# The dense mixer's down product with tokens held in the array and 512 weight columns moving, its sum copied, turned and added at the change of layers

## The chip, the core and the metric

The kernel runs on one core of one Trainium2 chip. The metric is the device time of one execution in microseconds (us). Below, PE is TensorE's matmul side and PEld its load of the operand that is held in the array, DVE is VectorE, ACT is ScalarE, POOL is GpSimd and SP the engine that issues most DMAs. Each engine runs its own instruction list in order; the lists meet only at semaphores (`wait_ge` waits for a count, `then_inc` raises one). Nothing overtakes a waiting instruction on its own engine.

## What is computed

Two residual layers over 256 tokens with 1024 channels; layer 0 ends in a dense SwiGLU, layer 1 in an expert SwiGLU. Cut to what matters here:

```python
D_MODEL, SEQ, DEPTH, D_FF = 1024, 256, 2, 2816

def swiglu(x, wg, wu, wd):
    return (jax.nn.silu(x @ wg) * (x @ wu)) @ wd

for layer in range(DEPTH):
    h = rmsnorm(x, norm1_g[layer])
    proj = h @ w_in[layer]            # the next layer begins with this
    ...                               # four mixers, gates, output projection
    h2 = rmsnorm(x, norm2_g[layer])
    f = swiglu(h2, ffn_wg, ffn_wu, ffn_wd) if layer % 2 == 0 else moe_ffn(...)
    x = x + f
```

The change is in `@ wd` of layer 0 and in the `x = x + f` behind it.

## The kernel before

**Data.** `x` lies in SBUF with channels on the 128 partitions: 8 tiles of 256 tokens, handled in four pairs (`PAIRS`). Weights come in units of 1 MB (128 x 2048), through three slots (`RING`). ACT copies a unit into a rounded part `weight_hi` (`split`, L441), DVE subtracts to get the rest `weight_lo` (`split`, L797). Activations are split into hi and lo in the same way, and a product is three matmuls (hi by hi, hi by lo, lo by hi), all recorded at L1525.

**The dense mixer** (`FF_STEPS` = 11 steps, three units each: gate, up, down). A step is `up_pair(4, ...)`, a down unit and `up_pair(6, ...)` on PE; nine of them are a loop, the last two are written out. ACT copies half of a gate or up sum out of PSUM (L652), DVE adds the other half (L1159), scales it (L1161), multiplies gate by up (L1172) and splits the product into `y_hi` (L1174) and `y_lo` (L800). `down(j)` then holds a 128 x 128 weight block in the array and moves the 256 tokens: 2 x 8 blocks x 3 = 48 matmuls of 256 columns a unit, summed over all steps in PSUM banks 0 to 3, two channel tiles to a bank. The units of the mixer are f0+0 to f0+32, the last two (f0+31, f0+32) both being down units.

**The change of layers.** In the last down unit (`down(..., final=True)`) the banks become ready one after another. DVE adds a bank to `x` (`added`, L938); ACT scales and rounds the pair for the next layer (`high`, L453) and squares it for the norm (`squares`, L458); DVE makes its lo part (`low`, L807), which raises `xg_lo_done`. PE begins the first unit of layer 1 (u = 0, `tile_pair` with `early` = 6), waiting for a count of `xg_lo_done` ahead of every second channel tile. The second unit (u = 1) needs `lo_done` of its weights: ACT's and DVE's splits of it are the last of the mixer's splits. In ACT's list its split stands ahead of the four `high`, in DVE's list behind the last `low`. Behind it DVE adds up the squares (`squares_added`, L814 and L815); PE sums them over partitions between u = 1 and u = 2 (`norm_sums`, a matmul of `proj` by `con`), and the norm's root and reciprocal follow (L463, L819).

**A step that exists already** is `merged_turned`: PE turns 128 x 128 blocks of an f32 tensor with tokens on partitions (`merged`, part of `proj`) by matmuls with the identity (`con`), L1622. It is used for the output projection. `wide_unit` is the product with tokens held and 512 weight columns moving, used in other units of the mixer layers.

Of the kernel before, what the change touches and what calls it, by code (L numbers as in the profile page):

```python
# [21 lines left out]
D = 1024  # L22
SEQ = 256
# [80 lines left out]
def trunk(nc, x_in, par_in, con_in, fin_in, mix_w, ff_w, moe_w, out, rows, made):  # L104
# [4 lines left out]
    with ctx:  # L109
# [164 lines left out]
        def hi_free(v, item):  # L274
# [18 lines left out]
            "y_done", "yz_done", "yb_sq_added", "yb_sum", "yb_std", "yb_recip", "yb_rstd", "ya_f", "ya_hi", "ya_lo", "yc_f",  # L293
            "yc_hi", "yc_lo", "yd_f", "yd_hi", "yd_lo", "yb_f", "yb_hi", "yb_lo", "early_ps", "gate_done", "early_added", "late_ps", "gate_b_done", "merge_done", "mT_ps",
            "m_hi", "m_lo", "half_copied", "g_scaled", "silu_done", "hid_done",
            "ff_bank", "y_bank", "xg_done", "xT_ps", "x_tok_done", "ssq_done", "pre_done",
# [136 lines left out]
        def _(act):  # L433
# [22 lines left out]
            def squares(q):  # L456

                A(flat(sq[:, 2 * q:2 * q + 2, :]), flat(x[:, 2 * q:2 * q + 2, :]), ACT.Square).then_inc(S["sq_done"], 1)  # L458
# [17 lines left out]
            def mixer_unit(layer, u, behind_split=None):  # L476
# [49 lines left out]
                elif U_PB + 2 <= u < U_OUT:  # L526
                    for q in (0, 1) if u == U_PB + 2 else (2, 3):
                        act.wait_ge(S["mT_ps"], PAIRS * layer + q + 1)
                        A(h_hi[:, 2 * q:2 * q + 2, :], tiles(bank(4 + q)), ACT.Copy).then_inc(S["m_hi"], 1)
                elif u > U_OUT and layer == 0:  # L530
                    high(1, u - U_OUT - 1)
                    squares(u - U_OUT - 1)
# [74 lines left out]
            for layer in range(DEPTH):  # L607
# [16 lines left out]
                else:  # L624
                    for q in range(PAIRS):
                        high(2 * layer, q)
                        squares(q)
                u = 0
# [9 lines left out]
                if layer == 0:  # L638
# [10 lines left out]
                    def half_copied(to, b, unit):  # L649

                        act.wait_ge(unit_used, RING + f0 + unit + 1)
                        A(tiles(to), PS[:, b:b + 2, 0:SEQ], ACT.Copy).then_inc(S["half_copied"], 1)  # L652

# [19 lines left out]
                    step(FF_STEPS - 2, True)  # L673
                    split(f0, FF_UNITS - 1 + AHEAD)

# [107 lines left out]
        def _(dve):  # L783
# [151 lines left out]

            def added(q):

                V.tensor_tensor(flat(x[:, 2 * q:2 * q + 2, :]), flat(x[:, 2 * q:2 * q + 2, :]), bank(q), ALU.add).then_inc(S["x_sum"], 1)  # L938

# [168 lines left out]
            for layer in range(DEPTH):  # L1108
# [38 lines left out]
                if layer == 0:  # L1147
# [8 lines left out]
                    def halves_scaled(out_, b, copied, signal, n):  # L1156

                        dve.wait_ge(S["half_copied"], copied)
                        V.tensor_tensor(tiles(out_), tiles(out_), PS[:, b:b + 2, SEQ:], ALU.add).then_inc(signal, 1)  # L1159
                        dve.wait_ge(signal, n + 1)  # L1160
                        V.tensor_tensor(tiles(out_), tiles(out_), rstd_pair, ALU.mult).then_inc(signal, 1)  # L1161
# [33 lines left out]
                    split(u + 2, AHEAD)  # L1195
                    for q in range(PAIRS):
                        if q < PAIRS - 1:
                            dve.wait_ge(S["ff_bank"], q + 1)
                        else:
                            dve.wait_ge(unit_used, RING + f0 + FF_UNITS)  # L1200
                        added(q)
                        if q:
                            low(2, q - 1)
                    low(2, PAIRS - 1)
                    split(u + 3, AHEAD)
# [317 lines left out]
        def _(pe):  # L1523
# [92 lines left out]
            def merged_turned(layer, n):  # L1616

                pe.wait_ge(S["merge_done"], TT * (HALVES * layer + n + 1))
                for k in range(4 * n, 4 * n + 4):
# [3 lines left out]
                    if k % 2:  # L1623
                        last.then_inc(S["mT_ps"], 1)

# [11 lines left out]
            def mixer_unit(layer, u):  # L1637
# [10 lines left out]
                elif u < IN_UNITS:  # L1648
# [9 lines left out]
                    elif layer == 0 and u == 1:  # L1658
                        pe.wait_ge(S["first_lo"], 4)
                        tile_pair(1, b, 1, a=xg, between=lambda n: split_is(1) if n == 0 else None)  # L1660
                    else:
                        tile_pair(u, b, u, (S["xg_lo_done"], 2 * PAIRS * layer) if u == 0 else None, 6 if u == 0 else KT, xg)
                elif u < U_GB:
# [160 lines left out]
            for layer in range(DEPTH):  # L1824
# [8 lines left out]
                if layer == 0:  # L1833
                    f0 = MIX_UNITS

                    def down(j, to=(hid_hi, hid_lo), final=False):

                        order = [(f, m) for f in range(2) for m in range(KT)]
                        if final:
                            order.sort(key=lambda fm: fm[1] // 2)  # L1840
                        for n, (f, m) in enumerate(order):
                            last = product(bank(m // 2)[:, (m % 2) * SEQ:(m % 2 + 1) * SEQ], (f0 + j) % RING, f * KT + m,
                                           to[0][:, f, :], to[1][:, f, :], False, False)
                            if final and n in (3, 7, 11):
                                last.then_inc(S["ff_bank"], 1)
                        last.then_inc(unit_used, 1)
# [23 lines left out]
                    pe.wait_ge(S["hid_done"], 5 * FF_STEPS - 5)  # L1870
                    down(u + 2)
                    split_is(f0 + u + 3)
                    pe.wait_ge(S["hid_done"], 5 * FF_STEPS)
                    down(u + 3, (last_hi, last_lo), True)

# [263 lines left out]
```

## Time and profile before

| | us |
|---|---|
| runs shown | 1823.03, 1823.12, 1824.83 (median 1823.12) |
| the profiled execution | 1824.91, its span 1823.0 |
| PE busy | 1809.2 (99%) |
| DVE, ACT busy | 1513.5 (83%), 1185.9 (65%) |
| dense mixer of layer 0 | about 342 to 522.8 |
| granted clock of TensorE, mean | 0.999 |

The span is from the first to the last recorded instruction; 1.9 us lie around it. Because matmuls overlap, the busy time of PE says little; what counts is the distance from the start of one matmul to the start of the next.

### The profile page before, as it was taken

The numbers are of one execution on the slowest core, as the hardware profiler recorded it, in microseconds if no ns is written. First come the engines' busy times: TensorE is split into PE (matmuls) and PEld (weight loads), VectorE is DVE, ScalarE is ACT, GpSimd is POOL, SyncE is SP. The second block draws the span as 40 slices with busy tenths as digits, with TensorE's granted clock in tenths as the row PEclk, the third lists the DMA queues.
The fourth block names the chain that finished last, engine by engine and source line by source line (L and its number), as shares of the span: only waits on it lengthen the run. The fifth ranks groups of instructions, "written<-read, shape, count | busy, mean of one in ns | idle before, by whom it ended". The sixth has DMA issues, their size and how long they took to land.

```text
span 1823.0 us, 25706 instructions
## 1 busy us (share of the span) xinstructions
PE 1809.2 (99%) x9443; PEld 1537.3 (84%) x9443; DVE 1513.5 (83%) x1372; ACT 1185.9 (65%) x1032; POOL 165.8 (9%) x143
## 2 busy tenths in 40 slices
PE   9999999999999999999999999999999999999997
PEld 7888888999998888879888888888888888888886
DVE  7887687866689867787989988898898898898897
ACT  5755554544456655656778777677677777777775
POOL 1044000000000350000920000000000000000010
PEclk9999999999999999999999999999999999999999
DMA  9554445555545454454999999999999999999994
GB/s 361 181 182 169 172 168 183 185 185 184 196 174 197 170 180 167 164 203 179 405 383 374 379 385 386 370 380 383 389 374 377 367 384 388 375 384 373 384 408 185
DMA packets 75229, 521.20 MB, mean 286 GB/s; under 512 B 8352, under 2 KB 8608, under 8 KB 14368
## 3 DMA queue, kind: packets, MB, share of 16 engines
q1 hardware_dynamic: 72112, 509.34, 74.1%
q0 software_dynamic: 2912, 11.01, 1.6%
q8 instruction: 42, 0.69, 0.1%
q14 instruction: 19, 0.16, 0.0%
q10 hardware_dynamic: 144, 0.00, 0.0%
HBM read 509.83 MB, written 10.49 MB: 285 GB/s over the span
## 4 chain that ended last, share of the span: by engine, by line
PE 96%; DVE 2%; DMA 1%; ACT 1%; issue 0%; ACTq 0%; SPq 0%; DVEq 0%
PE psum L1525 94%; PE psum L1999 1%; DMA weight_raw<-mix_w 0%; PE psum L1931 0%; DMA par<-par_in 0%; DVE yb_pair L807 0%; DVE weight_lo L797 0%; PE psum L1752 0%; PE psum L1622 0%; DVE rstd_row L819 0%; DVE proj L830 0%; DVE weight_lo L1104 0%; DVE h_pair L850 0%; DVE x L938 0%; ACT weight_hi L441 0%
## 5 line engine op out<-in xcount | busy, mean ns | idle before, releaser
L797 DVE TENSOR_TENSOR weight_lo<-weight_raw,weight_hi 128x2048 fp32r<-128x2048 f32 x139 | 319.9, 2302 | 107.0 <-ACT weight_hi L441 105.7
L441 ACT ACTIVATE weight_hi<-weight_raw 128x2048 fp32r<-128x2048 f32 x139 | 265.5, 1911 | 93.6 <-PE psum L1525 89.4
L1525 PE MATMUL psum<-weight_hi,y_hi 128*128 128x512 f32 x768 | 305.5, 398 | 0.6 <-DVE y_lo L1254 0.6
L1525 PE MATMUL psum<-weight_hi,y_lo 128*128 128x512 f32 x768 | 300.0, 391 | 0.0
L1525 PE MATMUL psum<-weight_lo,y_hi 128*128 128x512 f32 x768 | 298.9, 389 | 0.0
L1525 PE MATMUL psum<-weight_lo,y_lo 128*128 128x512 f32 x672 | 261.6, 389 | 0.0
L1525 PE MATMUL psum<-weight_raw_r,y_hi 128*128 128x512 f32 x576 | 224.6, 390 | 0.0
L1525 PE MATMUL psum<-proj_r,y_hi 128*128 128x512 f32 x576 | 224.3, 389 | 0.0
L1525 PE MATMUL psum<-h_pair,weight_hi 128*128 128x512 f32 (+1 forms) x928 | 203.2, 342 | 0.0
L850 DVE TENSOR_TENSOR weight_raw_r<-weight_raw,weight_lo 128x2048 fp32r<-128x2048 f32 x72 | 164.8, 2289 | 25.0 <-ACT weight_lo L474 24.7
L850 DVE TENSOR_TENSOR proj_r<-proj,weight_lo 128x2048 fp32r<-128x2048 f32 x72 | 164.9, 2290 | 24.5 <-ACT weight_lo L474 24.4
L1525 PE MATMUL psum<-weight_hi,h_pair 128*128 128x512 f32 x576 | 184.9, 393 | 0.0
L1525 PEld LDWEIGHTS psum<-h_pair,weight_hi 128*128 128x128 f32 x928 | 156.5, 190 | 17.6 <-issue 1.8
L1525 PEld LDWEIGHTS psum<-weight_hi,y_lo 128*128 128x128 f32 x768 | 144.1, 188 | 30.8
L850 DVE TENSOR_TENSOR weight_raw_r<-weight_raw,weight_hi 128x2048 fp32r<-128x2048 f32 x72 | 164.8, 2289 | 5.6 <-ACT weight_hi L474 5.2
L1525 PEld LDWEIGHTS psum<-weight_lo,y_hi 128*128 128x128 f32 x768 | 144.2, 188 | 29.9
L1525 PEld LDWEIGHTS psum<-weight_hi,y_hi 128*128 128x128 f32 x768 | 144.3, 188 | 28.8 <-DVE y_lo L1254 0.8
L850 DVE TENSOR_TENSOR proj_r<-proj,weight_hi 128x2048 fp32r<-128x2048 f32 x72 | 164.8, 2289 | 4.3 <-ACT weight_hi L474 4.2
L474 ACT ACTIVATE weight_hi<-weight_raw 128x2048 fp32r<-128x2048 f32 x72 | 138.2, 1920 | 30.0 <-DMA weight_raw<-moe_w 28.3
L474 ACT ACTIVATE weight_hi<-proj 128x2048 fp32r<-128x2048 f32 x72 | 138.8, 1927 | 20.8 <-DMA proj<-moe_w 17.8
L474 ACT ACTIVATE weight_lo<-weight_raw 128x2048 fp32r<-128x2048 f32 x72 | 137.7, 1912 | 19.9 <-DMA weight_raw<-moe_w 19.9
L1525 PEld LDWEIGHTS psum<-weight_lo,y_lo 128*128 128x128 f32 x672 | 126.1, 188 | 26.2
(316 smaller groups left out, 3115.6 us busy)
## 6 DMA issues: line engine op xcount, KB each, us to landing
proj<-moe_w SPq DMA_DIRECT2D x144, 1024.0 KB, 6.8
weight_raw<-moe_w SPq DMA_DIRECT2D x144, 1024.0 KB, 6.7
weight_raw<-mix_w SPq DMA_DIRECT2D x106, 1024.0 KB, 4.8
first_raw<-moe_w SPq DMA_DIRECT2D x48, 1024.0 KB, 6.7
weight_raw<-ff_w SPq DMA_DIRECT2D x33, 1024.0 KB, 4.7
made_rows<-zeros POOLq DMA_DIRECT2D x1, 4096.0 KB, 20.7
made_rows<-pool_tmp SPq DMA_DIRECT2D x8, 512.0 KB, 6.2
weight_raw<-mix_w SPq DMA_DIRECT2D x4, 512.0 KB, 8.5
```

The source lines that it names most:

```text
L441: A(hi[:, slot, :], raw[:, slot, :], ACT.Copy).then_inc(hi_done, 1)
L474: A(hi_e(v), raw_e(v), ACT.Copy).then_inc(hi_done, 1)
L797: V.tensor_tensor(lo[:, slot, :], raw[:, slot, :], hi[:, slot, :].bitcast(f32), ALU.subtract).then_inc(lo_done, 1)
L850: V.tensor_tensor(lo_e(v), raw_e(v), hi_e(v).bitcast(f32), ALU.subtract).then_inc(lo_done, 1)
L1525: return nc.tensor.matmul(o, a, b_, start=start, stop=stop, skip_group_check=True, **k)
L1999: last = nc.tensor.transpose(bank(6)[:, f * P:(f + 1) * P], ff_h[:, f * P:(f + 1) * P], C_("ident"))
```

## The change

The down product swaps its operands: a 128-token block of the hidden rows is held and 512 columns of the weights move, so a unit is 2 x 2 x 2 x 3 = 24 matmuls of 512 columns. The sum now has tokens on partitions, one bank for each half of the channels (`n`) and token block (`t`). So before `x` can take it, ACT copies each bank to SBUF (`ff_kept`), PE turns it in 16 blocks (`ff_turned`, eight at a time) into banks 4 to 7, and DVE adds from there. `ff_turned(0)` stands ahead of the last two parts of the last unit, `ff_turned(1)` inside the first unit of layer 1, which now has `early` = 4. In the last two units parts are interleaved. ACT's split of unit u = 1 of layer 1 moves behind the last `squares`. The semaphores `mT_ps` and `half_copied` are renamed.

```diff
@@ scalar, start of layer 1
-                    for q in range(PAIRS):
-                        high(2 * layer, q)
-                        squares(q)
+                    def ff_kept(n, t):
+                        if n and t:
+                            act.wait_ge(unit_used, RING + MIX_UNITS + FF_UNITS)
+                        else:
+                            act.wait_ge(S["ff_bank"], TT * n + t + 1)
+                        A(merged[:, t, cols(n)], bank(2 * n + t), ACT.Copy).then_inc(S["ff_copied"], 1)
+
+                    ff_kept(0, 0)
+                    ff_kept(0, 1)
+                    high(2, 0)
+                    ff_kept(1, 0)
+                    high(2, 1)
+                    ff_kept(1, 1)
+                    squares(0)
+                    squares(1)
+                    high(2, 2)
+                    high(2, 3)
+                    squares(2)
+                    squares(3)
+                    split(MIX_UNITS, FF_UNITS - 1 + AHEAD)
@@ scalar, end of the mixer
-                    split(f0, FF_UNITS - 1 + AHEAD)
@@ vector, end of the mixer
-                    for q in range(PAIRS):
-                        if q < PAIRS - 1:
-                            dve.wait_ge(S["ff_bank"], q + 1)
-                        else:
-                            dve.wait_ge(unit_used, RING + f0 + FF_UNITS)
-                        added(q)
-                        if q:
-                            low(2, q - 1)
-                    low(2, PAIRS - 1)
+                    for half in range(2):
+                        for q in (2 * half, 2 * half + 1):
+                            dve.wait_ge(S["turned_ps"], PAIRS + q + 1)
+                            added(q, 4)
+                        low(2, 2 * half)
+                        low(2, 2 * half + 1)
@@ tensor
+            def ff_turned(n):
+                pe.wait_ge(S["ff_copied"], 2 * FF_STEPS + TT * (n + 1))
+                for k in range(4 * n, 4 * n + 4):
+                    for t in range(TT):
+                        at = (k % 2) * SEQ + t * P
+                        last = nc.tensor.transpose(bank(4 + k // 2)[:, at:at + P], merged[:, t, k * P:(k + 1) * P], C_("ident"))
+                    if k % 2:
+                        last.then_inc(S["turned_ps"], 1)
@@ tensor, units of a mixer layer
+                    elif u == 0:
+                        tile_pair(0, b, 0, (S["xg_lo_done"], 2 * PAIRS * layer), 4, xg, lambda n: ff_turned(1) if n == 0 else None)
                     else:
-                        tile_pair(u, b, u, (S["xg_lo_done"], 2 * PAIRS * layer) if u == 0 else None, 6 if u == 0 else KT, xg)
+                        tile_pair(u, b, u, a=xg)
@@ tensor, the down unit
+                    def down_part(j, to, n, t):
+                        slot = (f0 + j) % RING
+                        for f in range(2):
+                            w = slice(f * D + 512 * n, f * D + 512 * n + 512)
+                            mm(bank(2 * n + t), to[0][:, f, token(t)], hi[:, slot, w], False, False)
+                            mm(bank(2 * n + t), to[0][:, f, token(t)], lo[:, slot, w], False, False)
+                            last = mm(bank(2 * n + t), to[1][:, f, token(t)], hi[:, slot, w], False, False)
+                        return last
@@ tensor, the last two down units
-                    down(u + 2)
+                    rows_a, rows_b = (hid_hi, hid_lo), (last_hi, last_lo)
+                    down_part(u + 2, rows_a, 0, 0)
+                    down_part(u + 2, rows_a, 0, 1)
+                    down_part(u + 2, rows_a, 1, 0)
                     split_is(f0 + u + 3)
                     pe.wait_ge(S["hid_done"], 5 * FF_STEPS)
-                    down(u + 3, (last_hi, last_lo), True)
+                    down_part(u + 3, rows_b, 0, 0).then_inc(S["ff_bank"], 1)
+                    down_part(u + 3, rows_b, 0, 1).then_inc(S["ff_bank"], 1)
+                    down_part(u + 2, rows_a, 1, 1).then_inc(unit_used, 1)
+                    ff_turned(0)
+                    down_part(u + 3, rows_b, 1, 0).then_inc(S["ff_bank"], 1)
+                    down_part(u + 3, rows_b, 1, 1).then_inc(unit_used, 1)
```

ACT's list at the change of layers, before: from the last copy of an up sum (L652) to the norm's table load. The row with x2 at L441 holds the splits of the first two units of layer 1.

```order
L652 ACTIVATE proj<-psum 128x512
L441 ACTIVATE weight_hi<-weight_raw 128x2048 x2
L453 ACTIVATE yb_pair<-x,par 128x256 x2
L458 ACTIVATE proj<-x 128x512
L453 ACTIVATE yb_pair<-x,par 128x256 x2
L458 ACTIVATE proj<-x 128x512
L453 ACTIVATE yb_pair<-x,par 128x256 x2
L458 ACTIVATE proj<-x 128x512
L453 ACTIVATE yb_pair<-x,par 128x256 x2
L458 ACTIVATE proj<-x 128x512
L441 ACTIVATE weight_hi<-weight_raw 128x2048 x2
L463 ACT_TABLE_LOAD
```

The same place of the changed kernel, where L670 is the copy of an up sum and L631 is `ff_kept`.

```order
L670 ACTIVATE proj<-psum 128x512
L441 ACTIVATE weight_hi<-weight_raw 128x2048
L631 ACTIVATE proj<-psum 128x512 x2
L453 ACTIVATE yb_pair<-x,par 128x256 x2
L631 ACTIVATE proj<-psum 128x512
L453 ACTIVATE yb_pair<-x,par 128x256 x2
L631 ACTIVATE proj<-psum 128x512
L458 ACTIVATE proj<-x 128x512 x2
L453 ACTIVATE yb_pair<-x,par 128x256 x4
L458 ACTIVATE proj<-x 128x512 x2
L441 ACTIVATE weight_hi<-weight_raw 128x2048 x3
L463 ACT_TABLE_LOAD
```

One of the two splits ahead of `high` has moved behind the last `squares`, and the second `high` stands behind the third `ff_kept`.

DVE's list at the same place, before (L797 split, L938 `added`, L807 `low`, L814 and L815 `squares_added`).

```order
L797 TENSOR_TENSOR weight_lo<-weight_raw,weight_hi 128x2048
L938 TENSOR_TENSOR x<-x,psum 128x512 x2
L807 SCALAR_TENSOR_TENSOR yb_pair<-x,par,yb_pair 128x256 x2
L938 TENSOR_TENSOR x<-x,psum 128x512
L807 SCALAR_TENSOR_TENSOR yb_pair<-x,par,yb_pair 128x256 x2
L938 TENSOR_TENSOR x<-x,psum 128x512
L807 SCALAR_TENSOR_TENSOR yb_pair<-x,par,yb_pair 128x256 x4
L797 TENSOR_TENSOR weight_lo<-weight_raw,weight_hi 128x2048
L814 TENSOR_TENSOR proj<-proj 128x512 x3
L815 TENSOR_TENSOR proj<-proj 128x256
L797 TENSOR_TENSOR weight_lo<-weight_raw,weight_hi 128x2048 x2
L819 RECIPROCAL rstd_row<-rstd_row 128x256
```

And of the changed kernel (L814 is the split there, L955 `added`, L824 `low`, L831 and L832 `squares_added`).

```order
L814 TENSOR_TENSOR weight_lo<-weight_raw,weight_hi 128x2048
L955 TENSOR_TENSOR x<-x,psum 128x512 x2
L824 SCALAR_TENSOR_TENSOR yb_pair<-x,par,yb_pair 128x256 x4
L955 TENSOR_TENSOR x<-x,psum 128x512 x2
L824 SCALAR_TENSOR_TENSOR yb_pair<-x,par,yb_pair 128x256 x4
L814 TENSOR_TENSOR weight_lo<-weight_raw,weight_hi 128x2048
L831 TENSOR_TENSOR proj<-proj 128x512 x3
L832 TENSOR_TENSOR proj<-proj 128x256
L814 TENSOR_TENSOR weight_lo<-weight_raw,weight_hi 128x2048 x2
L836 RECIPROCAL rstd_row<-rstd_row 128x256
```

The additions come in twos, and DVE's split of unit u = 1 keeps its place.

## Rows read from the trace of the kernel before

**Rows 1.** The page: busy times and shares; the chain that ended last, by engine.

```profile
PE 1809.2 (99%) x9443; PEld 1537.3 (84%) x9443; DVE 1513.5 (83%) x1372; ACT 1185.9 (65%) x1032; POOL 165.8 (9%) x143
...
PE 96%; DVE 2%; DMA 1%; ACT 1%; issue 0%; ACTq 0%; SPq 0%; DVEq 0%
```

**Rows 2.** Timeline of PE, dense mixer: start, length in us, engine, line, operation, tiles, count.

```profile
359.05 2.00 PE L1525 MATMUL psum<-yb_pair,weight_hi 128*128 128x512 f32 x8
...
370.22 0.28 PE L1525 MATMUL psum<-y_hi,weight_hi 128*128 128x256 f32 x1
...
375.98 2.00 PE L1525 MATMUL psum<-yb_pair,weight_hi 128*128 128x512 f32 x8
```

**Rows 3.** Timeline of PE, a `wide_unit` of layer 0, first and last of 24.

```profile
240.04 0.39 PE L1525 MATMUL psum<-weight_hi,y_hi 128*128 128x512 f32 x1
...
245.25 0.39 PE L1525 MATMUL psum<-weight_hi,y_lo 128*128 128x512 f32 x1
```

**Rows 4.** Timeline of PE around `merged_turned` of layer 0.

```profile
305.50 1.03 PE L1622 MATMUL psum<-con,proj 128*128 128x128 f32 x8
306.29 0.48 PE L1525 MATMUL psum<-weight_hi,yb_pair 128*128 128x512 f32 x1
306.60 0.40 PE L1525 MATMUL psum<-weight_lo,yb_pair 128*128 128x512 f32 x1
```

**Rows 5.** Timeline of ACT, first reader of the turned tiles.

```profile
306.13 1.09 ACT L529 ACTIVATE h_pair<-psum 128x512 fp32r<-128x512 f32 x2 [3.90 <-PE psum L1622]
```

**Rows 6.** Timeline of PE at the change of layers.

```profile
511.28 0.28 PE L1525 MATMUL psum<-y_hi,weight_hi 128*128 128x256 f32 x1
...
522.80 0.40 PE L1525 MATMUL psum<-yb_pair,weight_hi 128*128 128x256 f32 x2
...
524.53 0.51 PE L1525 MATMUL psum<-yb_pair,weight_hi 128*128 128x256 f32 x2
524.87 0.28 PE L1525 MATMUL psum<-yb_pair,weight_lo 128*128 128x256 f32 x1
...
534.71 0.59 PE L1525 MATMUL psum<-proj,con 128*128 128x256 f32 x2
```

**Rows 7.** Timeline of DVE at the change of layers.

```profile
514.75 0.69 DVE L800 TENSOR_TENSOR y_lo<-proj,y_hi 128x512 fp32r<-128x512 f32 x1
...
518.68 0.69 DVE L938 TENSOR_TENSOR x<-x,psum 128x512 f32<-128x512 f32 x1 [1.04 <-PE psum L1525]
...
520.72 0.87 DVE L807 SCALAR_TENSOR_TENSOR yb_pair<-x,par,yb_pair 128x256 fp32r<-128x256 f32 x2
...
525.46 2.28 DVE L797 TENSOR_TENSOR weight_lo<-weight_raw,weight_hi 128x2048 fp32r<-128x2048 f32 x1
527.66 2.14 DVE L814 TENSOR_TENSOR proj<-proj 128x512 f32<-128x512 f32 x3
...
530.18 4.49 DVE L797 TENSOR_TENSOR weight_lo<-weight_raw,weight_hi 128x2048 fp32r<-128x2048 f32 x2
537.18 1.75 DVE L819 RECIPROCAL rstd_row<-rstd_row 128x256 f32<-128x256 f32 x1 [2.52 <-ACT rstd_row L463]
```

**Rows 8.** Timeline of ACT at the change of layers.

```profile
511.48 0.60 ACT L652 ACTIVATE proj<-psum 128x512 f32<-128x512 f32 x1 [2.61 <-PE psum L1525]
...
517.29 1.92 ACT L441 ACTIVATE weight_hi<-weight_raw 128x2048 fp32r<-128x2048 f32 x1 [3.41 <-PE psum L1525]
519.46 0.91 ACT L453 ACTIVATE yb_pair<-x,par 128x256 fp32r<-128x256 f32 x2 [0.25 <-DVE x L938]
520.28 0.62 ACT L458 ACTIVATE proj<-x 128x512 f32<-128x512 f32 x1
```

**Rows 9.** DVE in the loop, the last split of a hidden product ahead of the down unit at 370.22.

```profile
368.19 0.69 DVE L800 TENSOR_TENSOR y_lo<-proj,y_hi 128x512 fp32r<-128x512 f32 x1
```

**Rows 10.** Stretches at the end: us, busy times (counts), granted clock, DMA share, GB/s.

```profile
1816.00:1818.00 2.00, 0.00 (x0) 0.00 (x0) 1.97 (x6) 1.37 (x5) 0.00 (x0) 1.00 0.00 0
1818.00:1820.00 2.00, 0.00 (x0) 0.00 (x0) 0.94 (x2) 1.13 (x2) 0.00 (x0) 0.60 0.31 116
```

**Rows 11.** DMA issues from 500 to 560: KB each, median us from issue to landing.

```profile
weight_raw<-mix_w SPq DMA_DIRECT2D x10, 1024.0 KB, 4.8
```

More of the change, by code:

```diff
@@ L293, in trunk @@
             "y_done", "yz_done", "yb_sq_added", "yb_sum", "yb_std", "yb_recip", "yb_rstd", "ya_f", "ya_hi", "ya_lo", "yc_f",
-            "yc_hi", "yc_lo", "yd_f", "yd_hi", "yd_lo", "yb_f", "yb_hi", "yb_lo", "early_ps", "gate_done", "early_added", "late_ps", "gate_b_done", "merge_done", "mT_ps",
-            "m_hi", "m_lo", "half_copied", "g_scaled", "silu_done", "hid_done",
+            "yc_hi", "yc_lo", "yd_f", "yd_hi", "yd_lo", "yb_f", "yb_hi", "yb_lo", "early_ps", "gate_done", "early_added", "late_ps", "gate_b_done", "merge_done", "turned_ps",
+            "m_hi", "m_lo", "ff_copied", "g_scaled", "silu_done", "hid_done",
             "ff_bank", "y_bank", "xg_done", "xT_ps", "x_tok_done", "ssq_done", "pre_done",
@@ L527, in mixer_unit @@
                     for q in (0, 1) if u == U_PB + 2 else (2, 3):
-                        act.wait_ge(S["mT_ps"], PAIRS * layer + q + 1)
+                        act.wait_ge(S["turned_ps"], 2 * PAIRS * layer + q + 1)
                         A(h_hi[:, 2 * q:2 * q + 2, :], tiles(bank(4 + q)), ACT.Copy).then_inc(S["m_hi"], 1)
@@ L651, in half_copied @@
                         act.wait_ge(unit_used, RING + f0 + unit + 1)
-                        A(tiles(to), PS[:, b:b + 2, 0:SEQ], ACT.Copy).then_inc(S["half_copied"], 1)
+                        A(tiles(to), PS[:, b:b + 2, 0:SEQ], ACT.Copy).then_inc(S["ff_copied"], 1)
                     def step(i, last):
@@ L934, in into_experts, with added @@
                 last.then_inc(S["xg_done"], 1)
-            def added(q):
-                V.tensor_tensor(flat(x[:, 2 * q:2 * q + 2, :]), flat(x[:, 2 * q:2 * q + 2, :]), bank(q), ALU.add).then_inc(S["x_sum"], 1)
+            def added(q, first=0):
+                V.tensor_tensor(flat(x[:, 2 * q:2 * q + 2, :]), flat(x[:, 2 * q:2 * q + 2, :]), bank(first + q), ALU.add).then_inc(S["x_sum"], 1)
             def stage(name, layer):
@@ L1156, in halves_scaled @@
                     def halves_scaled(out_, b, copied, signal, n):
-                        dve.wait_ge(S["half_copied"], copied)
+                        dve.wait_ge(S["ff_copied"], copied)
                         V.tensor_tensor(tiles(out_), tiles(out_), PS[:, b:b + 2, SEQ:], ALU.add).then_inc(signal, 1)
@@ L1623, in merged_turned @@
                     if k % 2:
-                        last.then_inc(S["mT_ps"], 1)
+                        last.then_inc(S["turned_ps"], 1)
[6 more added lines that the diff above has]
+                    if k % 2:
+                        last.then_inc(S["turned_ps"], 1)
             def out_half(layer, q, n):
@@ L1834, in _, with down @@
                     f0 = MIX_UNITS
[L1836 to L1845, printed above, removed]
+                    def down_part(j, to, n, t):
[6 more added lines that the diff above has]
+                        return last
+                    def down(j):
+                        for n in range(2):
+                            for t in range(TT):
+                                last = down_part(j, (hid_hi, hid_lo), n, t)
                         last.then_inc(unit_used, 1)
```

## Prediction

> **What bounds the kernel.** I read the page first: PE is busy 99% of the span, and the chain that ended last lies 96% on PE [rows 1]. That leaves open whether PE waits between its matmuls, so I read its timeline in the mixer. One turn of the loop is 359.05 to 375.98, 16.93 us. The down unit fills 370.22 to 375.98: 5.76 us for 48 matmuls, 0.120 us from start to start, and the next up product follows at once [rows 2]. PE waits for nobody in the loop, so what shortens its list there shortens the kernel, as long as the others keep up. They do: the hidden product of the down unit at 370.22 is ready at 368.19 + 0.69 = 368.88, 1.3 us early [rows 9], and it is timed from the up product in front of it, which does not change.
>
> The second place to read is the change of layers, because the changed sum has to pass three engines there. From the start of the second-last down unit, 511.28, to the norm's sum behind unit u = 1, 534.71, PE takes 23.43 us [rows 6]. That is four units of 5.76 and about 0.4 of waiting and restart at 524.53. I take 511.28 as zero in what follows, and the norm's sum as the end of the place, since all later work of DVE and ACT on layer 1 is timed from it.
>
> **The matmuls.** Before, a down unit costs 5.76 us. After, it is 24 matmuls of 512 columns with tokens held. The trace has this form in `wide_unit`: 24 of them, the first at 240.04 and the last at 245.25, so 5.21 / 23 = 0.2265 us from start to start [rows 3]. A unit is 5.44, a saving of 0.32 us. Nine down units are in the loop: **-2.9 us**. The other two are in the place that I work out as a whole. All eleven would be -3.5.
>
> The Trainium skill (TensorE: Matmul & The Clock Gate, "Back-to-back issue gap") gives N / 2.4 + 2.5 ns for isolated matmuls, 109 and 216 ns, by which a unit would go from 5.24 to 5.18 us, an estimate from that page. The trace disagrees: it shows 120 and 226.5 ns. The same section gives 131 ns a matmul of 512 columns for a sustained stream, by which the unit would fall to 3.14 us, again an estimate; no row of this f32 stream is near it.
>
> **The turning.** Eight transposes take PE from 305.50 until normal pace is back: the second matmul behind them starts at 306.60 and would have started 0.23 after the first, so 306.60 - 305.50 - 0.23 = 0.87 us [rows 4]. Sixteen cost 1.75 us of PE, which nothing hides. The first reader of a turned pair starts at 306.13, 0.63 after the first transpose [rows 5].
>
> **The place, step by step** (us after the start of the second-last down unit; 6 matmuls of 512 columns are 1.36):
> - Three parts of the second-last unit end at 4.1. The last part `rows_b` needs the last hidden product, which is ready at 514.75 + 0.69 - 511.28 = 4.16 [rows 7]; that wait was hidden behind the full unit before, and now costs 0.1 and a restart of 0.1 (the row pair 524.53 and 524.87 is 0.34 apart instead of 0.24 [rows 6]). Parts (0,0), (0,1) and the held-back (1,1) then end at 8.4. The ACT copies of the first two banks, 0.60 each and starting 0.2 after PE leaves a bank [rows 6, 8], are done by 7.9, so `ff_turned(0)` runs at once, 8.4 to 9.3.
> - Part (1,0) ends at 10.6. On ACT the second `high` stands behind the copy of this bank: copy 10.8 to 11.4, `high` 0.91 to 12.3 [rows 8], `low` 0.87 on DVE to 13.2 [rows 7]. PE has ended the last part at 12.0 and the first two channel tiles of u = 0 at 12.7, and waits 0.5 for the second pair. The tiles end at 14.0.
> - `ff_turned(1)` runs 14.0 to 14.9 (its copies are long done). Its first pair is read at 14.6: add 0.69 to 15.3, `high` to 16.2, `low` to 17.1 [rows 7, 8]. PE spends 1.44 on the other four tiles, is through at 16.4, waits 0.8, and for the fourth pair another 0.1, which ends at 18.0. Unit u = 0 ends at 20.3.
> - **ACT's split of unit u = 1 is late.** Before, it ran at 517.29, that is at 6.0 [rows 8], and only DVE's part (525.46 to 527.74) came after the lows [rows 7]. Now ACT does it behind all `high` and `squares`: the last `high` ends at 17.1, two `squares` of 0.62 to 18.3, the split 1.92 to 20.2, DVE's split 2.28 to 22.5. PE wants the unit at 20.3 and waits **2.2 us**. Unit u = 1 with a restart ends at 28.4.
>
> Full lengths overstate such a chain a little, since the next instruction of an engine starts up to 0.1 ahead of the listed end (520.28 is 0.82 after 519.46, listed 0.91 [rows 8]). With five such steps I take 28.3; the bounds are 27.5 (all overlap, no restarts) and 29.0 (0.1 for each semaphore). So the place goes from 23.4 to 28.3: **+4.9 us**. As a check on PE alone: two units save 0.6, turning costs 1.75, waits and restarts 4.2 where there were 0.4.
>
> **What is late next.** DVE's list behind its split is `squares_added` (527.66 to 530.18, 2.5 us) and the splits of u = 2 and u = 3 (4.5) [rows 7]; they end at 22.5 + 7.0 = 29.5. The reciprocal of the norm comes 537.18 - 534.71 = 2.5 after the norm's sum [rows 6, 7], at 30.8, so 1.3 us of slack is left, and nothing more is paid. Unit u = 2 has its lo part at 27.2, ahead of 28.4. SP's load for unit u = 4 waits for `lo_done` of u = 1: issued at 22.5, it lands 4.8 later at 27.3 [rows 11], while ACT splits it behind the norm's root, after 30. The loads of u = 2 and u = 3 hang on earlier units. POOL has no part here.
>
> **Sum.** -2.9 + 4.9 = +2.0 us: the profiled execution of 1824.91 would become 1826.9. That execution is 1.8 above the median of the runs, 1823.12, so the median I expect is **1825.1 us**. A measurement of this kernel can tell some 0.2% (3.6 us) from no change, so this is no change that counts. The likeliest case's own range is 1823.9 to 1826.4.
>
> **Rivals.**
> - *The chain at the change of layers is covered* (0.13). If the splits and lows overlap more than I have it, only matmuls and turning are left: -3.5 + 1.75 = -1.8, so 1821.3. For it: PE has matmuls to do during most of the steps. Against it: ACT's list fixes copy, `high`, `squares` and split behind each other, and 2.2 us of wait would have to be hidden by nothing.
> - *Slower by more than can be missed: the clock falls in the waits* (0.07). PE stands still for 0.5, 0.9 and 2.2 us within 12 us. At the end of the trace the granted clock is still 1.00 in a stretch with no matmul, and 0.60 in the next [rows 10], so it has come down from 2.4 to 1.2 GHz there once PE had stopped for good. If it fell ahead of u = 1, its 48 matmuls would take twice 5.76: +5.8, so 1830.9. It decides as soon as some 14 matmuls of 0.12 run at half pace. Against it: in the stretch from 1816 to 1818 PE did nothing at all and the clock was still 1.00, and the waits here are of that length or shorter, with matmuls between them.
> - *The work behind the change of layers piles up* (0.13). If DVE's split ends 1.3 us later than I have it, the norm's reciprocal is late and with it the projection's scale, and each later microsecond is paid: +3 to +4.5 in all, 1826.5 to 1827.6.
> - *The wide form saves nothing* (0.04). If moving the columns were all that a matmul costs, 24 of 512 columns would take as long as 48 of 256, 5.76 us: nothing in the loop, and +4.9 to +5.5 at the change, so about 1828.3. Against it: 0.2265 is less than twice 0.120 [rows 2, 3], with the same types. The Trainium skill's rule for isolated matmuls (same page and section as above) comes near this case, with 0.06 us a unit, again an estimate from it.
> - *As forecast* (0.63).
>
> **How the numbers follow.** No case reaches faster by 0.2%: all eleven units together save 3.5 us before a single transpose is paid. I leave 0.03 for what I have not seen. Slower by 0.2% means above 1826.8: the clock case, about half of the pile-up and the case without saving, together 0.17. The range from 1821.5 to 1828.0 leaves out the clock case, the case without saving and a little at the lower end, together under 0.2.
>
> **What would show it.** Right: down units of 24 matmuls in 5.44 us; a loop turn of 16.6; eight transposes in 0.9 us twice; PE waiting for `low` inside u = 0, and for DVE's split ahead of u = 1, by 2 us; the place from the second-last down unit to the norm's sum at 28.3 us; the same distances from there on. Wrong: a wait of PE inside the loop, a granted clock under 1.00 in or behind the place, or waits of DVE or PE for the norm that grow. An error of more than 1 us in the time of DVE's split of u = 1 would move the result one for one.

## The result, and the profile after

The changed kernel took 1826.86 us in the median of 19 runs (1824.61 to 1830.35), the kernel before 1823.41 in as many (1822.68 to 1827.31). The ratio is 1.0016, with an interval of 1.0010 to 1.0022: slower by 2.9 us by the ratio and by 3.45 us by the medians, clear of the noise, but under the 0.2% set in the forecast. The range and the sign hold. The forecast of +2.0 us was 0.9 to 1.4 us short, and the forecast median of 1825.1 was 1.8 us short, 0.3 of it because it starts from the three runs shown (median 1823.12, where 19 runs give 1823.41). The fastest runs of the two kernels lie 1.93 us apart.

The page of the changed kernel, the row that answers to [rows 1]:

```profile
PE 1809.2 (99%) x9195; PEld 1526.5 (84%) x9195; DVE 1512.5 (83%) x1372; ACT 1185.6 (65%) x1036; POOL 167.5 (9%) x143
```

PE is as busy as before with 248 matmuls fewer: 264 are gone, 16 transposes are new. The share tells nothing, so on to its timeline (start, length, engine, line, operation, tiles, count; L1539 is the matmul line now). First the loop, against [rows 2]:

```profile
351.94 0.40 PE L1539 MATMUL psum<-weight_hi,y_hi 128*128 128x512 f32 x1
...
357.41 1.98 PE L1539 MATMUL psum<-yb_pair,weight_hi 128*128 128x512 f32 x8
...
368.56 0.40 PE L1539 MATMUL psum<-weight_hi,y_hi 128*128 128x512 f32 x1
```

The down unit takes 357.41 - 351.94 = 5.47 us where it took 5.76, a turn 16.62 where it took 16.93. From this first down unit to the second-last one, at 507.05 below, are 155.11 us. Before, the first down unit started at

```profile
353.29 0.28 PE L1525 MATMUL psum<-y_hi,weight_hi 128*128 128x256 f32 x1
```

and the second-last one at 511.28 [rows 6], 157.99 us later. So the nine units of the loop give the 2.88 us of the forecast.

Then PE at the change of layers, against [rows 6]. L1646 is `ff_turned`:

```profile
507.05 0.40 PE L1539 MATMUL psum<-weight_hi,y_hi 128*128 128x512 f32 x1
...
511.35 0.47 PE L1539 MATMUL psum<-weight_hi,y_hi 128*128 128x512 f32 x1
...
515.55 1.03 PE L1646 MATMUL psum<-con,proj 128*128 128x128 f32 x8
516.35 0.48 PE L1539 MATMUL psum<-weight_hi,y_hi 128*128 128x512 f32 x1
...
520.38 0.50 PE L1539 MATMUL psum<-yb_pair,weight_hi 128*128 128x256 f32 x2 [0.32 <-DVE yb_pair L824]
...
521.20 1.04 PE L1646 MATMUL psum<-con,proj 128*128 128x128 f32 x8
...
524.44 0.51 PE L1539 MATMUL psum<-yb_pair,weight_hi 128*128 128x256 f32 x2 [0.77 <-DVE yb_pair L824]
...
529.50 0.50 PE L1539 MATMUL psum<-yb_pair,weight_hi 128*128 128x256 f32 x2 [1.84 <-DVE weight_lo L814]
...
530.54 0.63 PE L1539 MATMUL psum<-yb_pair,weight_hi 128*128 128x256 f32 x2
530.97 0.41 PE L1539 MATMUL psum<-yb_pair,weight_lo 128*128 128x256 f32 x1
531.18 0.63 PE L1539 MATMUL psum<-yb_pair,weight_hi 128*128 128x256 f32 x2
...
536.84 0.59 PE L1539 MATMUL psum<-proj,con 128*128 128x256 f32 x2
```

The three waits stand in brackets where the forecast put them: for the second pair, for the third pair, and ahead of u = 1. On its scale of zero at the second-last down unit, u = 1 starts at 529.50 - 507.05 = 22.45 (forecast 22.5). But the norm's sum comes at 29.79, not at 28.3. The rows behind the third wait say why: a group of three matmuls of 256 columns begins 531.18 - 530.54 = 0.64 us after the one before it, where 0.36 is the pace elsewhere. The stretches of PE (width, then busy times and counts of PE, PEld, DVE, ACT, POOL; granted clock; DMA) show the clock:

```profile
528.00:530.00 2.00, 0.51 (x4) 0.51 (x5) 2.00 (x2) 2.00 (x2) 0.00 (x0) 1.00 0.00 0
530.00:532.00 2.00, 2.00 (x11) 2.00 (x11) 1.90 (x5) 0.71 (x1) 0.00 (x0) 0.50 0.65 164
532.00:534.00 2.00, 2.00 (x14) 2.00 (x13) 2.00 (x1) 0.00 (x0) 0.00 (x0) 0.64 0.86 356
534.00:536.00 2.00, 2.00 (x19) 2.00 (x18) 2.00 (x2) 0.00 (x0) 0.00 (x0) 1.00 0.34 53
```

PE has worked only 0.51 of the 2 us up to 530. The granted clock is 0.50 in the next stretch, 1.2 GHz instead of 2.4, and it is back at 1.00 about 3 us after it fell. ACT and DVE, against [rows 7, 8]; L631 is `ff_kept`, L453 `high`, L441 the split, L824 `low`, L814 DVE's split, L831 `squares_added`:

```profile
517.85 0.88 DVE L824 SCALAR_TENSOR_TENSOR yb_pair<-x,par,yb_pair 128x256 fp32r<-128x256 f32 x2 [0.38 <-ACT yb_pair L453]
...
527.15 2.29 DVE L814 TENSOR_TENSOR weight_lo<-weight_raw,weight_hi 128x2048 fp32r<-128x2048 f32 x1 [1.96 <-ACT weight_hi L441]
529.36 2.14 DVE L831 TENSOR_TENSOR proj<-proj 128x512 f32<-128x512 f32 x3
...
539.32 1.75 DVE L836 RECIPROCAL rstd_row<-rstd_row 128x256 f32<-128x256 f32 x1 [2.96 <-ACT rstd_row L463]
```

```profile
518.02 0.60 ACT L631 ACTIVATE proj<-psum 128x512 f32<-128x512 f32 x1 [0.20 <-PE psum L1539]
518.52 0.90 ACT L453 ACTIVATE yb_pair<-x,par 128x256 fp32r<-128x256 f32 x2
...
525.22 5.50 ACT L441 ACTIVATE weight_hi<-weight_raw 128x2048 fp32r<-128x2048 f32 x3
```

ACT begins the split of u = 1 at 525.22, 18.2 on the scale (forecast 18.3), where it began at 6.0 before; DVE ends its part at 22.4. Nothing piles up behind: the reciprocal follows the norm's sum by 2.48 us, as before by 2.47.

One more thing has to be known to compare single traces. This execution was 1.3 us ahead of the one of before already at its first transposes (74.38 against 75.71), because a weight load at the start landed earlier (ACT's split of the fourth weight unit began at 20.85 against 22.16). So its span is only 2.1 us longer (1825.1 against 1823.0), while loop and change of layers sum to -2.88 + 6.36 = +3.5. That this one sum meets the difference of the medians (3.45) is partly luck: an execution of the same code whose clock stays up sums to +2.0 (e6 below), and the runs hold both kinds.

### The profile page after: what moved, and what is told of

Same layout as the page of the kernel before. It is cut to its first block, busy times and chain, and to the rows that moved or that the text cites. A ratio compares the mean times of both kernels' runs of the same rounds, so it can differ in the third digit from the quotient of the medians.

```text
span 1825.1 us, 25214 instructions
## 1 busy us (share of the span) xinstructions
PE 1809.2 (99%) x9195; PEld 1526.5 (84%) x9195; DVE 1512.5 (83%) x1372; ACT 1185.6 (65%) x1036; POOL 167.5 (9%) x143
## 4 chain that ended last, share of the span: by engine, by line
PE 96%; DVE 2%; ACT 1%; DMA 1%; issue 0%; ACTq 0%; SPq 0%; DVEq 0%
PE psum L1539 94%; PE psum L2038 1%; DMA weight_raw<-mix_w 0%; DVE weight_lo L814 0%; PE psum L1970 0%; DMA par<-par_in 0%; ACT yb_pair L453 0%; ACT weight_hi L441 0%; PE psum L1778 0%; PE psum L1636 0%; DVE rstd_row L836 0%; DVE proj L847 0%; DVE yb_pair L824 0%; DVE weight_lo L1121 0%; DVE h_pair L867 0%
## 5 line engine op out<-in xcount | busy, mean ns | idle before, releaser
L814 DVE TENSOR_TENSOR weight_lo<-weight_raw,weight_hi 128x2048 fp32r<-128x2048 f32 x139 | 319.8, 2301 | 104.7 <-ACT weight_hi L441 103.4
L1539 PE MATMUL psum<-weight_hi,y_hi 128*128 128x512 f32 x856 | 340.0, 397 | 0.6 <-DVE y_lo L1268 0.6
L1539 PE MATMUL psum<-weight_hi,y_lo 128*128 128x512 f32 x856 | 334.3, 390 | 0.0
L1539 PE MATMUL psum<-weight_lo,y_hi 128*128 128x512 f32 x856 | 333.2, 389 | 0.0
L441 ACT ACTIVATE weight_hi<-weight_raw 128x2048 fp32r<-128x2048 f32 x139 | 265.2, 1910 | 86.0 <-PE psum L1539 81.2
L1539 PE MATMUL psum<-weight_lo,y_lo 128*128 128x512 f32 x672 | 261.6, 389 | 0.0
L1539 PE MATMUL psum<-weight_raw_r,y_hi 128*128 128x512 f32 x576 | 224.6, 390 | 0.0
L1539 PE MATMUL psum<-proj_r,y_hi 128*128 128x512 f32 x576 | 224.3, 389 | 0.0
L1539 PE MATMUL psum<-h_pair,weight_hi 128*128 128x512 f32 (+1 forms) x928 | 203.1, 342 | 0.0
L1539 PEld LDWEIGHTS psum<-weight_hi,y_lo 128*128 128x128 f32 x856 | 160.6, 188 | 34.3
L1539 PEld LDWEIGHTS psum<-weight_lo,y_hi 128*128 128x128 f32 x856 | 160.7, 188 | 32.9
L1539 PEld LDWEIGHTS psum<-weight_hi,y_hi 128*128 128x128 f32 x856 | 160.9, 188 | 32.3 <-DVE y_lo L1268 0.7
L1539 PE MATMUL psum<-weight_hi,h_pair 128*128 128x512 f32 x576 | 184.9, 393 | 0.0
L1539 PEld LDWEIGHTS psum<-h_pair,weight_hi 128*128 128x128 f32 x928 | 156.5, 190 | 17.7 <-issue 1.8
L1539 PEld LDWEIGHTS psum<-weight_lo,y_lo 128*128 128x128 f32 x672 | 126.1, 188 | 26.2
L713 ACT ACTIVATE y_hi<-psum 128x512 fp32r<-128x512 f32 x56 | 33.5, 598 | 175.3 <-PE psum L2038 175.3
```

What stands on the lines that cost most here:

```text
L441: A(hi[:, slot, :], raw[:, slot, :], ACT.Copy).then_inc(hi_done, 1)
L713: A(flat(turned(final, c)[0]), bank(6), ACT.Copy).then_inc(S["hT_hi_done"], 1)
L814: V.tensor_tensor(lo[:, slot, :], raw[:, slot, :], hi[:, slot, :].bitcast(f32), ALU.subtract).then_inc(lo_done, 1)
L1539: return nc.tensor.matmul(o, a, b_, start=start, stop=stop, skip_group_check=True, **k)
```

## Experiments

Each was timed in 11 runs, e8 in 6, beside runs of the kernel before on the same chip. "The place" is the distance from the second-last down unit to the norm's sum: 23.43 us before, 29.79 in the changed kernel's first trace. The sum that stands beside each is the place less 23.43 less 2.88 for the loop, if not said otherwise.

**e1, the split early.** 

```diff
                     high(2, 1)
                     ff_kept(1, 1)
-                    squares(0)
-                    squares(1)
+                    split(MIX_UNITS, FF_UNITS - 1 + AHEAD)
                     high(2, 2)
                     high(2, 3)
+                    squares(0)
+                    squares(1)
                     squares(2)
                     squares(3)
-                    split(MIX_UNITS, FF_UNITS - 1 + AHEAD)
```

> The changed kernel, with ACT's split of unit u = 1 of layer 1 put directly behind the last copy of the down sum, ahead of the third high; all four squares stand behind the fourth high. Theory A (two costs hang on the late split: PE's wait of 2.1 us with its restart, and 1.5 us of half clock that the wait brings on): PE reaches u = 1 without a wait, the granted clock stays 1.00 there, the place from the second-last down unit to the norm's sum takes 26.2 us instead of 29.8, the median is 1823.3, level with before. Theory B (the wait goes, but the clock falls anyway, because of the earlier waits and the transposes): 27.7 us for the place, 1824.8.

(The two squares move as well, behind the third and fourth `high`.) Measured: 1823.76 us against 1823.69, ratio 1.0002 (0.9993 to 1.0011). The second-last down unit and the norm's sum in PE's timeline:

```profile
507.58 0.40 PE L1539 MATMUL psum<-weight_hi,y_hi 128*128 128x512 f32 x1
...
533.82 0.59 PE L1539 MATMUL psum<-proj,con 128*128 128x256 f32 x2
```

The place takes 26.24, sum -0.1; no wait is left ahead of u = 1, and the granted clock is 1.00 from 520 to 540. This is theory A. The waits for the second and the third pair are still there (0.32 and 0.77 us), and the split, which starts at 520.42 now, fits into the time that ACT had spent on the two squares (1.14 us) and on waiting for DVE (1.53). So the loss against the kernel before hangs on the place of one line in ACT's list, for which the squares make room at no cost.

**e2, the wait filled.**

```diff
+                if layer and u == 1:
+                    idle(1, 8)
                 if u > 1 or layer:
                     split_is(b + u)
```

> The changed kernel, with eight matmuls of 512 columns that nobody reads placed in the wait ahead of unit u = 1 of layer 1 (1.8 us of PE work in a wait of 1.8 to 2.1 us). No wait is removed. Theory A (the empty stretch of PE brings the clock down in u = 1): granted clock 1.00 in u = 1, the unit takes 5.8 us instead of 7.3, median 1825.3, and the runs lie closer together than those of the changed kernel. Theory B (the fall comes from the earlier waits, the transposes or the chip's own state): u = 1 still shows half clock in part, median 1826.9 or more.

Measured: 1826.26 us against 1823.69, ratio 1.0012 (1.0003 to 1.0021), runs from 1825.03 to 1828.03. PE's timeline has the filling where the wait was, and then full pace:

```profile
507.03 0.40 PE L1539 MATMUL psum<-weight_hi,y_hi 128*128 128x512 f32 x1
...
527.49 1.99 PE L1539 MATMUL psum<-ones_r 128*128 128x512 f32 x8
...
535.33 0.59 PE L1539 MATMUL psum<-proj,con 128*128 128x256 f32 x2
```

The place takes 28.30, the number of the forecast, with PE doing useful work not a moment earlier than before. The median is 2.6 us over before; theory A has 1825.3, some 2 us over. The interval reaches over 2.0 and 3.5 alike, and e6 below, with nothing filled, comes to +1.8 on another chip. So no median shows what the filling saves; for the clock the traces and the mean clocks of the runs (below) have to decide.

**e6, the changed kernel again**, with no edit.

> The changed kernel once more, unchanged, on the chip of the three runs beside it. By the sum of its trace (nine units in the loop 2.9 us less, the place 29.8 us where it was 23.4) it comes to 3.5 us over the kernel before, if the clock falls as in its first profile; 2.0 if it doesn't. If the fall hangs on where the waits lie against the clock's own rhythm, single runs lie between these and above, with a wider spread than the kernel before.

Measured: 1826.33 us (1824.76 to 1828.81) against 1824.53, ratio 1.0010 (1.0001 to 1.0019). The same code, the same three waits, and no fall of the clock; PE's timeline and one of its stretches:

```profile
507.93 0.40 PE L1539 MATMUL psum<-weight_hi,y_hi 128*128 128x512 f32 x1
...
530.37 0.51 PE L1539 MATMUL psum<-yb_pair,weight_hi 128*128 128x256 f32 x2 [1.84 <-DVE weight_lo L814]
...
536.23 0.59 PE L1539 MATMUL psum<-proj,con 128*128 128x256 f32 x2
```

```profile
530.00:532.00 2.00, 1.63 (x13) 1.63 (x14) 1.93 (x4) 1.59 (x1) 0.00 (x0) 1.00 0.42 66
```

Again 28.30 us, sum +2.0. The fastest runs agree with it: 1824.61 and 1824.76 in the two sets of the changed kernel are 1.93 and 1.91 over the fastest of the kernel before beside them. Unit u = 1 takes 536.23 - 530.37 = 5.86 us here and 536.84 - 529.50 = 7.34 in the first trace, so the fall cost 1.5 us there. Each run also states its mean granted clock. Of the 30 runs of the changed kernel (19 and these 11) 14 had 0.999 and 16 had 0.997 or 0.998; of the 61 runs of the kernel before beside e1 to e9 50 had 0.999. In the first 19, those at 0.999 have a median of 1825.5, those at 0.998 of 1827.8, the two at 0.997 stand at 1829.6 and 1830.35. With e2's filling 10 of 11 runs are back at 0.999. The mean clock is a rough sign all the same: it doesn't say where the clock fell, and 11 of the 61 runs of the kernel before are under 0.999 too. Two traces show where else it falls. Every kernel here, the one before included, has two other waits of PE for DVE, one near 34 us (up to 1.8 us long) and one near 1804 (1.7 us in most). In the kernel before the clock was 1.00 behind both:

```profile
34.91 1.07 PE L1525 MATMUL psum<-proj,par 128*32 128x256 f32 x16 [1.68 <-DVE proj L830]
...
1803.65 0.66 PE L1999 MATMUL psum<-con,proj 128*128 128x128 f32 x4 [1.71 <-DVE proj L1267]
```

In the trace of e7 (below) it fell behind the first of them, in that of e9 behind the second, each time with a stretch close behind:

```profile
35.01 1.07 PE L1539 MATMUL psum<-proj,par 128*32 128x256 f32 x16 [1.81 <-DVE proj L847]
...
36.00:38.00 2.00, 2.00 (x15) 2.00 (x12) 2.00 (x5) 2.00 (x3) 0.00 (x0) 0.63 1.04 422
```

```profile
1806.01 0.66 PE L2038 MATMUL psum<-con,proj 128*128 128x128 f32 x4 [2.06 <-DVE proj L1281]
...
1808.00:1810.00 2.00, 2.00 (x6) 1.54 (x6) 1.22 (x2) 0.81 (x2) 0.00 (x0) 0.50 0.04 8
```

So 16 of 30 is not the count of falls at u = 1; the excess over 11 of 61 is nearer to what the change adds. Nor is the 2.3 us between the two groups of runs the price of one fall: a late weight load at the start delays a run and lengthens its wait near 34 us at once.

**e8, a longer wait**: one more ACT copy of a weight unit, with the two waits that it needs, into a tile that nobody reads, ahead of the late split.

```diff
                     squares(3)
+                    slot = (MIX_UNITS + FF_UNITS + 1) % RING
+                    act.wait_ge(raw_landed[slot], 16 * ((MIX_UNITS + FF_UNITS + 1) // RING + 1))
+                    act.wait_ge(unit_used, MIX_UNITS + FF_UNITS + 2)
+                    A(flat(y_hi[:, 4:12, :]), raw[:, slot, :], ACT.Copy)
                     split(MIX_UNITS, FF_UNITS - 1 + AHEAD)
```

> The changed kernel with one ACT copy of 128 x 2048 that nobody reads ahead of the late split, so that PE's wait ahead of u = 1 grows by 1.8 to about 3.9 us. Theory A (the clock falls because PE stands empty): it falls in the wait or in u = 1 in each run, half clock shows in u = 1, and the place takes 31.6 us (the same half-clock time as in the first profile) or more, 5.3 us or more over before. Theory F (only the waits cost, the slow matmuls were a chance of that one execution): full clock, 30.1 us, 3.8 us over before.

Measured: 1830.17 us (1828.48 to 1831.81) against 1824.53, ratio 1.0031 (1.0019 to 1.0044). PE's timeline (the matmul line is L1543 here) and a stretch behind the wait:

```profile
506.92 0.40 PE L1543 MATMUL psum<-weight_hi,y_hi 128*128 128x512 f32 x1
...
531.16 0.79 PE L1543 MATMUL psum<-yb_pair,weight_hi 128*128 128x256 f32 x2 [3.63 <-DVE weight_lo L818]
...
539.64 0.59 PE L1543 MATMUL psum<-proj,con 128*128 128x256 f32 x2
```

```profile
532.00:534.00 2.00, 2.00 (x11) 2.00 (x11) 1.93 (x4) 0.39 (x1) 0.00 (x0) 0.50 0.82 229
```

The place takes 32.72, of which u = 1 takes 8.48: 2.6 more than at full clock. All six runs have a mean clock of 0.997 or 0.998, where 6 of the 11 runs of e6 on the same chip had 0.999. This is theory A: the longer wait was paid twice, by its own length and by a fall that cost more; that it also comes more surely is what six runs suggest.

**e9, only the earlier wait filled**, the one for the third pair.

```diff
-  tile_pair(0, b, 0, (...), 4, xg, lambda n: ff_turned(1) if n == 0 else None)
+  tile_pair(0, b, 0, (...), 4, xg, lambda n: ff_turned(1) if n == 0 else idle(1, 3) if n == 1 else None)
```

> The changed kernel with three matmuls of 512 columns that nobody reads ahead of the third pair's wait (0.7 of 0.9 us), while the wait ahead of u = 1 stays empty. If the long wait alone brings the clock down, u = 1 still shows half clock and the median is that of the changed kernel, +3.5 us over before. If the waits count together, the fall is rarer or shorter: +2.0 to +2.5.

Measured: 1827.51 us (1825.12 to 1829.7) against 1824.53, ratio 1.0014 (1.0005 to 1.0023), +3.0. PE's timeline and the stretch behind its wait:

```profile
529.41 0.50 PE L1539 MATMUL psum<-yb_pair,weight_hi 128*128 128x256 f32 x2 [1.83 <-DVE weight_lo L814]
...
530.00:532.00 2.00, 2.00 (x14) 2.00 (x13) 1.93 (x4) 0.63 (x1) 0.00 (x0) 0.61 0.73 201
```

The clock is 0.53 in the stretch after that, and the place takes 29.78. Only 5 of 11 runs are at 0.999. So a wait of 1.8 us can be enough without the one for the third pair (the 0.31 us for the second pair stayed). Whether the earlier waits make the fall more frequent these runs can't tell.

**e5, the wide matmuls alone.** Without `ff_kept` and `ff_turned`, with the order of the kernel before at the change of layers. It leaves out the turning, so its output is not the reference's; only its time is read. The main lines of the edit:

```diff
-                            dve.wait_ge(S["turned_ps"], PAIRS + q + 1)
-                            added(q, 4)
+                        if q < PAIRS - 1:
+                            dve.wait_ge(S["ff_bank"], q + 1)
+                        else:
+                            dve.wait_ge(unit_used, RING + f0 + FF_UNITS)
+                        added(q)
...
-                    ff_turned(0)
```

> The changed kernel without copies and transposes: the down sum with tokens on partitions is added to x as it lies (so x is not the reference's from there on), high, squares, splits and the first unit of layer 1 are in the order of the kernel before. It shows what the wide matmuls alone give. Forecast by the prediction's term: eleven units by 0.32 us, 3.5 us less than before, 1819.9. Theory D (the wide form saves nothing outside the loop, since the chain behind it sets the time): 2.9 less, 1820.5. Theory E (the saving is lost to a new wait in the loop): level with before.

Measured: 1820.29 us against 1823.69, ratio 0.9980 (0.9971 to 0.9989), -3.4 us. PE's timeline:

```profile
507.26 0.40 PE L1533 MATMUL psum<-weight_hi,y_hi 128*128 128x512 f32 x1
...
530.13 0.59 PE L1533 MATMUL psum<-proj,con 128*128 128x256 f32 x2
```

The place takes 22.87, sum -3.4. The gain of the swap is real and whole (term: 3.5). Theory E falls by the median. Theory D (2.9) is nearer than the measurement can tell; the trace decides against it, since the place itself is 0.56 shorter.

**e4, the late split in the kernel before.**

```diff
                     for q in range(PAIRS):
                         high(2 * layer, q)
                         squares(q)
+                    split(MIX_UNITS, FF_UNITS - 1 + AHEAD)
@@ end of the mixer
-                    split(f0, FF_UNITS - 1 + AHEAD)
```

> The kernel before, with one part of the change alone: ACT's split of unit u = 1 of layer 1 stands behind the last squares. Theory A (the late split costs much only because the copies, transposes and highs ahead of it are late too): ACT's split at about 525.1 to 527.0, DVE's until 529.2, PE wants it at 528.9 and waits 0.3 us: 1823.8. Theory C (the place of the split in ACT's list is what costs, whatever stands around it): 2 us of wait, 1825.5 or more.

Measured: 1824.41 us against 1823.69, ratio 1.0003 (0.9994 to 1.0012). PE's timeline (the sum here is the place less 23.43):

```profile
510.37 0.28 PE L1525 MATMUL psum<-y_hi,weight_hi 128*128 128x256 f32 x1
...
528.43 0.50 PE L1525 MATMUL psum<-yb_pair,weight_hi 128*128 128x256 f32 x2 [0.23 <-DVE weight_lo L797]
...
534.28 0.59 PE L1525 MATMUL psum<-proj,con 128*128 128x256 f32 x2
```

A wait of 0.23 and a place of 23.91, +0.5. The late split alone costs next to nothing; it needs the longer chain of copies and transposes ahead of it to become 2.1 us (28.30 - 26.24). This is theory A.

**e7 and e10, the chain shortened.** e1, and:

```diff
                     high(2, 0)
-                    ff_kept(1, 0)
                     high(2, 1)
+                    ff_kept(1, 0)
                     ff_kept(1, 1)
@@ tensor, unit u = 0: ff_turned(1) behind two channel tiles, not four
-  tile_pair(0, b, 0, (...), 4, xg, lambda n: ff_turned(1) if n == 0 else None)
+  for n, (t, ks) in enumerate(((0, (0, 1)), (0, (2, 3)), (1, range(4)), (0, range(4, KT)), (1, range(4, KT)))):
+      ...
+      if n == 0:
+          ff_turned(1)
```

> The kernel of e1 with two more moves: the second high stands ahead of the third copy on ACT, and the second eight transposes stand behind the first two channel tiles of u = 0 instead of behind four. Expected by the chain: PE no longer waits for the second pair (0.4 us with its restart), and the transposes start 1.1 us earlier, so that the wait of 0.8 us for the third pair shrinks to about 0.1; the place takes 25.1 us, the total is 1.2 us under the kernel before, 1822.3. Rival: the waits move to the fourth pair or to u = 1 (DVE's split is behind the lows), and it stays level with e1 and with before.

Measured: 1822.69 us against 1824.53, ratio 0.9992 (0.9983 to 1.0001). The place takes 25.36 in its trace, where 25.1 was expected; a wait of 0.27 us for the third pair is left. That execution took 1825.29, the slowest of its eleven, with the fall near 36 us shown above.

> The kernel of e7 once more, to tell whether it beats the kernel before. Its trace says 0.95 us less: nine units in the loop save 2.88 us, the place takes 25.36 us where it was 23.43. If that is all, the ratio is 0.9995 and can hardly be told from 1; e7's own 0.9992 would be partly luck. If the ratio comes out at 0.999 or less again, the chain of waits is not the whole account.

Measured: 1823.42 us against 1823.54, ratio 0.9995 (0.9986 to 1.0004). PE's timeline in e10:

```profile
508.02 0.40 PE L1539 MATMUL psum<-weight_hi,y_hi 128*128 128x512 f32 x1
...
524.54 0.50 PE L1539 MATMUL psum<-yb_pair,weight_hi 128*128 128x256 f32 x2 [0.27 <-DVE yb_pair L824]
...
533.39 0.59 PE L1539 MATMUL psum<-proj,con 128*128 128x256 f32 x2
```

The place takes 25.37 with one short wait left, sum -0.94, which is a ratio of 0.9995. By the place it is faster than the changed kernel by 2.9 us, and e7's median was 3.6 under that of e6 on the same chip. That it beats the kernel before is what the traces say and what neither interval settles.

## Why the prediction was right, and where it was short

- *The loop saves 2.9 us.* It saved 2.88, and the spacing of 0.2265 us read off `wide_unit` [rows 3] nearly held for the down product (5.25 / 23 = 0.228 in the first unit shown). e5 shows the whole term: 3.4 us measured, 3.5 forecast.
- *Sixteen transposes cost 1.75 us of PE.* 515.55 to the second matmul behind them was again 0.9. Nothing hid them, as said.
- *ACT's split of u = 1 is late, and PE waits 2.2 us for it.* It started at 18.2 on the scale against 18.3, DVE ended at 22.4 against 22.5, PE waited 1.84 us and restarted. e1 removes this wait, e4 shows that the move is harmless without the chain ahead of it.
- *The place takes 28.3 us.* It did, to the hundredth, in e6 and in e2, but only when the clock stayed up. In the first trace it took 29.79.
- *The clock falls in the waits* was a rival with 0.07, at +5.8 us on top. What the forecast had wrong is there. The fall is neither so rare nor so dear: it was there in one of two traces of the changed kernel and cost 1.5 us, since the clock came back within u = 1. I made it all or nothing, a whole unit at half pace; and I took the stretch without matmuls at the end of the trace [rows 10] as if it showed that waits of this length are safe. The trace of before even had two nearer rows, the waits of 1.68 and 1.71 us shown under e6, both with full clock behind them, and they would have misled in the same way: in e7 and e9 the clock fell at these very places. One wait that ended well tells nothing of the next. The term should have been in the sum as a likely cost, not beside it.
- How much of the missing 0.9 to 1.4 us is the clock's stays open. At full clock the forecast is met (28.30, and 1.93 and 1.91 us between the fastest runs), so the rest comes from executions that differ. A fall of 1.5 us in a third of the runs, an estimate from 16 of 30 less 11 of 61, would be 0.5 us in the mean. The spread of the weight loads at the start is the other difference that the traces show, and no run separates the two.
- The Trainium skill (TensorE: Matmul & The Clock Gate, "HAM oscillation — how this bites in real kernels") tells of a kernel in which PE waits for a DMA after each group of matmuls, with waits longer than the 1.84 us here, and starts every next group at half clock. The traces agree in part: behind a wait of 3.63 us the clock was 0.50, but the fall also came behind a shorter wait of 1.84 us, and not each time, for the same code had 0.50 in one execution and 1.00 in another.
- *The work behind piles up.* It did not; the reciprocal kept its distance of 2.5 us from the norm's sum, and DVE stood idle for 1.47 us ahead of it in e6 (forecast 1.3).
- *The chain is covered* is what e1 makes true on purpose, and then the result is level with before, as -2.88 + 2.81 says.

## What to carry to other kernels

A swap of operands that makes fewer and wider matmuls is worth its fixed cost per matmul (here 0.2265 us for 512 columns in one matmul, 0.24 in two, 3.4 us in all), and it must be set against what the turned layout needs: transposes, copies, and a longer chain at the point where the sum is used. When a chain gets longer, look through each engine's list for work that stands behind it and doesn't belong to it: here one weight split, whose place decided between +3.5 and 0 us. And count a wait of TensorE like the 1.84 us here at more than its length, with a share for a fall of the clock behind it. A mean clock over a whole run says that the clock fell, not where; read the stretches behind each long wait.

## What the runs showed of the hardware

- With the same instructions and the same waits (1.84 us), the granted clock behind the wait was 0.50 in one execution and 1.00 in another. In the eleven traces the clock fell at the end of, or just behind, waits of 1.81, 1.83, 1.84, 2.06 and 3.63 us. It stayed at 1.00 behind the other wait of 1.84 us and behind 13 waits of 1.62 to 1.77 us. These are single executions, and no limit is drawn from them.
- Single runs of the changed kernel spread over 5.7 us (1824.61 to 1830.35), those of the kernel before beside them over 4.6, those with the wait filled over 3.0.
- Once fallen, it cost 1.5 us behind a wait of 1.8, and 2.6 behind one of 3.6.
- Executions differ by up to 1.6 us in their first 30 us: ACT's split of the fourth weight unit (L441) started between 20.68 (e8) and 22.26 (e7), waiting for its load. With full clock there, the place came out the same within 0.01 us (28.30 in e2 and e6, 25.36 in e7 and 25.37 in e10), while the spans differed, so places are better compared by distances than by spans.
